# Sample attention: VectorE and ScalarE one pair of slots behind TensorE, and VectorE copying two of four page banks

## What is computed

```
def mla_attend(q_lat, q_pe, ckv, kpe, ckv_past, kpe_past):
    ...
        sp = (jnp.einsum('bqhr,bkr->bhqk', ql, ckv_past)
              + jnp.einsum('bqhd,bkd->bhqk', qp, kpe_past)).astype(jnp.float32) * MLA_SCALE
        p = jax.nn.softmax(jnp.concatenate([sp, s], axis=-1), axis=-1).astype(ckv.dtype)
    ...
def peer(h, w_q, sub_keys, u_tab, v_tab):
    ...                      # top 16 of 16384 experts, for 8 heads
        act = jax.nn.gelu(jnp.einsum('td,thkd->thk', xb, u_tab[ib]), approximate=False) * gb
        return jnp.einsum('thk,thkd->td', act, v_tab[ib])
```

## Time and profile before

| | us |
|---|---|
| median of 3 runs | 3596.35 |
| lowest, highest | 3595.26, 3619.91 |
| the profiled execution | 3605.23 |
| its span | 3603.4 |

### The profile page before, as it was taken

The page is one execution under the profiler, slowest core; times in us unless marked ns, Lnnn a source line. Parts: engine busy times, 40 slices in busy tenths (PEclk is TensorE's granted clock), DMA queues, the critical chain, the costliest instruction groups (busy, mean ns, idle before and its releaser), DMA issues. The chain is left out here.

```text
span 3603.4 us, 44291 instructions
## 1 busy us (share of the span) xinstructions
PE 2576.4 (71%) x15271; PEld 1136.2 (32%) x15271; DVE 2175.5 (60%) x5407; ACT 1593.2 (44%) x4435; POOL 1195.2 (33%) x1114
## 2 busy tenths in 40 slices
PE   8987776666788875766656888866767666656566
PEld 7644222111334432322232443422323322221121
DVE  4863667767776776545345778866454454455566
ACT  3122444444555663244433557744444444444344
POOL 0210444444443443333213344433222222222343
PEclk9988776766898997776777999988888778776687
DMA  4115999999999999898759999999888788888998
GB/s 158 46 32 190 411 426 426 422 427 427 418 400 421 422 420 396 359 370 308 278 214 384 408 421 421 423 406 368 328 330 302 288 309 304 294 295 314 417 426 362
DMA packets 215854, 1240.70 MB, mean 344 GB/s; under 512 B 28015, under 2 KB 63503, under 8 KB 72773
## 3 DMA queue, kind: packets, MB, share of 16 engines
q0 software_dynamic: 154368, 1128.34, 77.5%
q1 hardware_dynamic: 59965, 108.63, 8.2%
q10 hardware_dynamic: 1296, 0.90, 0.1%
HBM read 1233.79 MB, written 4.46 MB: 344 GB/s over the span
## 5 line engine op out<-in xcount | busy, mean ns | idle before, releaser
L1782 PE MATMUL p_acc<-p_rows,p_diag 64*64 64x512 f32 x8192 | 1390.5, 791 | 865.7 <-ACT p_diag L1303 850.3
L1177 POOL DMA_INDIRECT p_rows<-in_peer_uv,p_ids x1024 | 1102.3, 1076 | 2036.6 <-PE p_acc L1782 1886.7
L1569 DVE CUSTOM_DVE_ANT_0 p_rows<-p_rows,p_x_n 128x1024 f32<-128x1024 f32 x1040 | 1248.5, 1221 | 491.6 <-DMA p_rows<-in_peer_uv,p_ids 479.5
L1782 PEld LDWEIGHTS p_acc<-p_rows,p_diag 64*64 64x64 f32 x8192 | 288.3, 159 | 1655.2 <-ACT p_diag L1303 1477.5
L1297 ACT ACTIVATE p_acts<-p_dots 128x1 f32<-128x1 f32 x1040 | 209.2, 201 | 1038.7 <-DVE p_dots L1569 1035.0
L1303 ACT ACTIVATE p_diag<-p_unit,p_gated 128x64 f32<-128x64 f32 x1024 | 356.0, 348 | 33.5
L1299 ACT ACTIVATE p_gated<-p_acts,p_gates 128x1 f32<-128x1 f32 x1024 | 301.7, 295 | 33.3
L1717 PE MATMUL p_q_banks<-p_xT,p_w_q 128*128 128x256 f32 (+3 forms) x1152 | 245.0, 374 | 22.9 <-DMA p_keys<-in_keysT 14.5
L1717 PEld LDWEIGHTS p_q_banks<-p_xT,p_w_q 128*128 128x128 f32 x1152 | 210.1, 204 | 57.9 <-issue 30.9
L1297 ACT ACT_TABLE_LOAD x142 | 182.2, 1283 | 5.9 <-DVE p_dots L1569 3.4
L2665 DVE TENSOR_REDUCE s_peak<-r_bank 128x1 f32<-128x256 f32 x32 | 13.6, 424 | 178.3 <-PE r_bank L2854 178.3
(11 more groups left out here) (417 smaller groups left out, 2787.3 us busy)
## 6 DMA issues: line engine op xcount, KB each, us to landing
p_w_q<-in_w_q_heads SPq DMA_DIRECT2D x35, 1024.0 KB
p_rows<-in_peer_uv,p_ids POOLq DMA_INDIRECT x1024, 14.2
r_arena<-in_c_w_out SPq DMA_DIRECT2D x8, 1024.0 KB, 24.7
a_w_in<-in_ab_w_in SPq DMA_DIRECT2D x6, 1024.0 KB, 11.7
r_arena<-in_w_qx SPq DMA_DIRECT2D x16, 384.0 KB, 12.6
r_arena<-in_c_w_in SPq DMA_DIRECT2D x2, 2688.0 KB, 13.0
r_arena<-in_w_q_heads SPq DMA_DIRECT2D x5, 1024.0 KB, 23.8
p_keys<-in_keysT SPq DMA_DIRECT2D x35, 128.0 KB
```

The costliest lines, as they stand in the source:

```text
L1177: nc.gpsimd.indirect_dma_start(out=rows[:, slot % RING, :], out_offset=None, in_=w[f"peer_uv{layer}"], in_offset=bass.IndirectOffsetOnAxis ...
L1569: nc.vector.tensor_tensor_reduce(rows[:, k % RING, 0:D_MODEL], rows[:, k % RING, 0:D_MODEL], x, 1.0, 0.0, ALU.mult, ALU.add, dots[:, slot ...
L1782: last = nc.tensor.matmul(acc[64 * c:64 * c + 64, 512 * r:512 * r + 512], diag[of, slot // GROUP % 4, j, :], rows[of, (slot + j) % RING, a ...
```

## The change

- The step lists of VectorE and ScalarE for the sample attention begin with one empty step. From then on each is one pair of slots behind TensorE's: what TensorE writes behind pair h, they take behind pair h + 1.
- `turn_weights` and `weighted` move one step later (to steps 4 + 1 and 5 + 1), and with them `weights_out` and `add_piece`, which thereby come two pairs later than before.
- VectorE copies both right-hand page banks (steps 0 and 1); ScalarE's `right_page_out` is gone. The two semaphores for the right bank become one.
- The merge comes one step later, uses `banks[1]` (the right-hand bank) and not `banks[2]`; its waits are on the page copies, and the next `turn_pages` of the right bank waits for it, not `scores`.
- The output of layer 1's round comes one step later; layer 0's round has two steps more, so that its last steps run after the last pair.

The diff, cut to its core:

```diff
-        assert att["stages"] + smp_att["stages"] <= GROUPS * (NW - ROUND_AT if layer == 0 else SMP_X)
+        assert att["stages"] + smp_att["stages"] < (GROUPS * (NW - ROUND_AT) + 4 if layer == 0 else GROUPS * SMP_X)
...
-    OUT_AT = LAST_AT + 11
-    STAGES = LAST_AT + 10 if rnd == 0 else OUT_AT + 7
+    OUT_AT = LAST_AT + 12
+    STAGES = LAST_AT + 12 if rnd == 0 else OUT_AT + 7
...
-    top_row, bias_col, total_col, fold_out = banks[2][0:1, 0:128], banks[2][:, 0:1], banks[2][:, 0:1], banks[2][:, 0:2 * H_C]
+    top_row, bias_col, total_col, fold_out = banks[1][0:1, 0:128], banks[1][:, 0:1], banks[1][:, 0:1], banks[1][:, 0:2 * H_C]
...
-        return SETUP + 4 * last + 6 + step * (4 if last + 1 < NPC else 1)
+        return SETUP + 4 * last + 7 + step * (4 if last + 1 < NPC else 1)
...
-            if rnd == 1 and s == LAST_AT + 6:
+            if rnd == 1 and s == LAST_AT + 7:
                 sp.wait_ge(o_ps, NPC)
...
-        def right_page_out(p):
-            act.wait_ge(right_ps, 2 * p + 2)
-            nc.scalar.copy(pagesT[:, :, 6:8, :], banks[1][:, :].rearrange("p (c s n) -> p c s n", c=2, s=2)).then_inc(right_act, 1)
...
+        yield
         for s in range(STAGES):
...
-            if (p := piece_at(s, 4)) is not None:
+            if (p := piece_at(s, 5)) is not None:
                 weights_out(p)
...
-        def page_out(p):
-
-            dve.wait_ge(right_ps, 2 * p + 1)
+        def page_out(p, r):
+
+            dve.wait_ge(right_ps, 2 * p + r + 1)
             if p:
                 dve.wait_ge(s_ps, p)
-            nc.vector.tensor_copy(pagesT[:, :, 2:4, :], banks[1][:, :].rearrange("p (c s n) -> p c s n", c=2, s=2)).then_inc(right_dve, 1)
+            nc.vector.tensor_copy(pagesT[:, :, 4 * r + 2:4 * r + 4, :], banks[1][:, :].rearrange("p (c s n) -> p c s n", c=2, s=2)).then_inc(right_out, 1)
...
+        yield
         for s in range(STAGES):
...
-            if (p := piece_at(s, 5)) is not None:
+            if (p := piece_at(s, 6)) is not None:
                 add_piece(p)
-            if (p := piece_at(s, 0)) is not None:
-                page_out(p)
+            for r in range(2):
+                if (p := piece_at(s, r)) is not None:
+                    page_out(p, r)
...
-            if r == 1:
-                pe.wait_ge(right_dve, p + 1)
-            elif p:
-                pe.wait_ge(right_act, p)
-            turn_page(banks[1], p, 4 * r + 2, right_ps)
...
+            if p or r:
+                pe.wait_ge(right_out, 2 * p + r)
+            if r == 0 and p > PAST_PIECES:
+                i, step = divmod(p - PAST_PIECES - 1, PAST_PIECES)
                 if step == 0:
                     pe.wait_ge(mx_ready, i + 1)
...
         def turn_top(i):
-            pe.wait_ge(o_used, outs_before(i, 0))
+            pe.wait_ge(top_step, 3 * (PAST_PIECES * i + PAST_PIECES))
+            pe.wait_ge(right_out, 2 * turned_before(i, 0))
...
-            if (p := piece_at(s, 4)) is not None:
+            if (p := piece_at(s, 5)) is not None:
                 turn_weights(p)
-            if (p := piece_at(s, 5)) is not None:
+            if (p := piece_at(s, 6)) is not None:
                 weighted(p)
```

More of the change, by code:

```diff
@@ L1102, in buffer_of, with hooked @@
             return x_n[:, t % 3, :]
-        def hooked(n):
+        def hooked(n, g):
             return n >= ROUND_AT if layer == 0 else n < SMP_X
@@ L1146, in _ @@
                         sp.dma_start(keys[:, 0].rearrange("p c n -> p (c n)"), w["keysT"][layer][:, D_KEY * (H_P - 1):D_KEY * H_P]).then_inc(w_q_in[0], 16)
-                    if n >= 0 and hooked(n):
+                    if n >= 0 and hooked(n, g):
                         next(steps, None)
@@ L1196, in _ @@
                     gather(first_slot(n) + k, ids[:, n % (AHEAD + 1), k:k + 1])
-                    if hooked(n) and k % GROUP == GROUP - 1:
+                    if k % GROUP == GROUP - 1 and hooked(n, k // GROUP):
                         next(steps, None)
@@ L1407, in _ @@
                         exps(route_no(m))
-                    if hooked(n):
+                    if hooked(n, g):
                         next(steps, None)
@@ L2450, in sample_round @@
         oT_ps, oT_ready, y_ps, y_used = sem("oT_ps"), sem("oT_ready"), sem("y_ps"), sem("y_used")
-    left_ps, left_out, right_ps, right_act, right_dve, qpb_ready = (sem(n) for n in (
-        "left_ps", "left_out", "right_ps", "right_act", "right_dve", "qpb_ready"))
+    left_ps, left_out, right_ps, right_out, qpb_ready = (sem(n) for n in (
+        "left_ps", "left_out", "right_ps", "right_out", "qpb_ready"))
     s_ps, top_step, e_ready, pT_ps, pT_ready, o_ps, l_step, o_used = (sem(n) for n in (
@@ L2477, in merge_at, with turned_before @@
         return None
-    def outs_before(i, step):
-        return min(PAST_PIECES * i + PAST_PIECES + step, NPC)
+    def turned_before(i, step):
+        return min(PAST_PIECES * i + PAST_PIECES + 1 + step, NPC)
     def old_top(p):
@@ L2612, in scalar_steps @@
                     left_page_out(p, r)
-            if (p := piece_at(s, 1)) is not None:
-                right_page_out(p)
             if (p := piece_at(s, 2)) is not None:
@@ L2813, in turn_pages @@
             turn_page(banks[0], p, 4 * r, left_ps)
-            if r == 1:
-                pe.wait_ge(right_dve, p + 1)
-            elif p:
-                pe.wait_ge(right_act, p)
+            if p or r:
+                pe.wait_ge(right_out, 2 * p + r)
+            if r == 0 and p > PAST_PIECES:
+                i, step = divmod(p - PAST_PIECES - 1, PAST_PIECES)
+                if step == 0:
+                    pe.wait_ge(mx_ready, i + 1)
+                if step == 1:
+                    pe.wait_ge(bias_out, i + 1)
+                if step == 2:
+                    pe.wait_ge(inv_step, 2 * i + 1)
+                if step == 3:
+                    pe.wait_ge(olT_ready, i + 1)
             turn_page(banks[1], p, 4 * r + 2, right_ps)
@@ L2829, in scores @@
             pe.wait_ge(left_out, 3 * p + 3)
-            pe.wait_ge(right_act, p + 1)
-            pe.wait_ge(right_dve, p + 1)
+            pe.wait_ge(right_out, 2 * p + 2)
             pe.wait_ge(qpb_ready, p // PAST_PIECES + 1)
@@ L2836, in scores @@
                 pe.wait_ge(self_ready, 1)
[L2837 to L2846, removed]
             b = ROUND_SEQS[p // PAST_PIECES]
@@ L2878, in spread_top @@
             pe.wait_ge(nmx_ready, i + 1)
-            pe.wait_ge(o_used, outs_before(i, 1))
+            pe.wait_ge(right_out, 2 * turned_before(i, 1))
             nc.tensor.matmul(bias_col, nmx[:].rearrange("p j h -> p (j h)"), one[:], start=True, stop=True).then_inc(bias_ps, 1)
@@ L2885, in total_sums @@
             pe.wait_ge(consts_in, 48)
-            pe.wait_ge(o_used, outs_before(i, 2))
+            pe.wait_ge(right_out, 2 * turned_before(i, 2))
             nc.tensor.matmul(total_col, fold[:], share[:, 2:3], start=True, stop=True).then_inc(total_ps, 1)
@@ L2890, in fold_heads @@
             pe.wait_ge(on_ready, i + 1)
-            pe.wait_ge(o_used, outs_before(i, 3))
+            pe.wait_ge(right_out, 2 * turned_before(i, 3))
             for c in range(2):
```

## The result

| | before | changed | ratio, 95% interval |
|---|---|---|---|
| median us | 3605.38 (4 runs) | 3296.99 (4 runs, 3291.43 to 3300.95) | 0.9141, 0.9100 to 0.9182 |
| span of the profiled execution, us | 3603.4 | 3295.1 | |

The change made the kernel 8.6% faster. The forecast had the direction and the mechanism, but its time of 3355 us is 58 us too long, and the low end of its range, 3300 us, lies 3 us above the measured median. The kernel before was measured at 3605.38 us in this comparison, 9 us over the 3596.35 that the forecast started from, so the saving was 308 us and the forecast's 242: it is 66 us short.

A forecast was written before the change was run, and what follows sets the result against it. Sample-attention stages were taken as bound by mutual engine waits, not transfers. 279 saved at 420 GB/s, less 48, plus 14, less 3 gives 242 us off 3605.2, so 3363 profiled, 3354 as median, stated 3355; range 3300 to 3435.

The forecast's parts named there:

- The circle: Sample attention: VectorE and TensorE wait for each other in turn, 8.2 us a pair; with the lag this stops setting the pace.
- the list of signs: Layer 1's stage: VectorE's waits from 340 to under 100 us, gather waits, 390 GB/s or more, about 600 us, clock 0.85 or higher.
- TensorE's room and imperfect overlap: 48 us given back: 16 blocks holding the pieces: 3 us lost each; bounds nothing at clock 0.92, about 6 us per query block at the old clock.
- The transfers' floor: 279 us: Both sample stages at 420 GB/s: layer 1's saves 212 us, layer 0's 67, the most this edit can give.
- VectorE's second copy: Sample attention: 22 us more on VectorE, hidden under the transfers; 22 us if that cover is gone.
- `weighted` a pair later: GpSimd's gather of past rows waits for this later step: 0 taken, at most 96 us.
- Merge and the end of layer 0: Last merge of each round saves 7 us, 14 in all; layer 0's steps after the last pair lose 3 us.
- Half of the waits stay: Sample stages: lag too short, TensorE's 358 us of waits for diagonals only halve; 179 us saved, 3417 us; chance 0.16.
- 370 GB/s: Sample stages can't move bytes at 420, only 370 to 376 GB/s at DMA share 1.0; 3407 us; chance 0.12.
- The wait moves to `exps`: ScalarE's `exps`, waiting for VectorE at its own pair, holds the next diagonals and keeps TensorE late; 3585 us; chance 0.05.
- GpSimd held: Gather of past rows waits for `weighted` behind a late TensorE, expert gathers queue behind, slots run dry; 3780 us; chance 0.03.
- The rule on HBM's 358 GB/s: Both sample stages: HBM binds at about 358 GB/s a core; 145 us saved, time near 3490 us; not taken.

The follow-up runs named there:

- e4: Changed kernel with the one-pair lag taken from ScalarE's steps except `exps`, VectorE's kept: 3375.66 us, 0.9305 of the kernel before.
- e5: Changed kernel without the lag for VectorE's page copies, `maxima`, `add_piece` and three merge steps, ScalarE's kept: 3611.84 us, 0.9955 of the kernel before.
- e6: Changed kernel with 26 of the 32 gathers of past rows each replaced by a 2 KB transfer: 3226.33 us, 71 us under the changed kernel.
- e7: Kernel before with the same 26 gathers of past rows left out: 3609.12 us, 1.0009 of the kernel before.
- e10: Changed kernel with each page transpose done four times: 3293.15 us, 0.9144 of the kernel before.
- e11: Changed kernel with a ring of 6 gather buffers instead of 8: 3411.20 us, 0.9468 of the kernel before.
- e1: Changed kernel with the second right-hand page copy given back to ScalarE, lag kept: 3298.07 us, 0.9095 of the kernel before.
- e2: Kernel before with both right-hand page copies on VectorE and no lag: 3674.68 us, 1.0130 of the kernel before.
- e3: Changed kernel with `turn_weights`, `weighted`, `weights_out` and `add_piece` one step earlier, the first two at steps 4 and 5: 3292.98 us, 0.9136 of the kernel before.
- e8: Changed kernel with each page transpose done twice: 3292.53 us, 0.9130 of the kernel before.
- e9: Kernel before with each page transpose done twice: 3667.56 us, 1.0161 of the kernel before.

## Why the prediction was right in kind and too cautious in size

- *The circle.* Right. VectorE's waits for TensorE fell from 340.6 us to 35.5, as the list of signs had asked (under 100), waits for gathers appeared, the rate is 424, the round 555 us, the clock 0.88. Taking either lag away brings waits and time back (e4, e5), and e6 with e7 shows that the bound changed to the transfers. Two readings were loose: VectorE had one wait for a gather in layer 1's stage (0.6 us) where I said none, and of "slices 18 to 20" the first runs at 370 GB/s, outside the 278 to 330 given.
- *TensorE's room and imperfect overlap: 48 us given back.* This is the step that failed: the runs show 0. I read "89% of 575" and "46.6 of 47.5 us in a block with queries" as no room. But 46.6 us do fit into 47.5; the 6 us of the dearer bound are what the experts' matmuls of a block cost more at the lower clock, not a time by which a block overran, and 3 us a block is half of that. Two things were wrong behind it. TensorE can be busy 92% of a stage and cost nothing (e10: 510 us of 554). TensorE's bursts in the blocks with queries are carried by the ring of 8 buffers (with 6 buffers those blocks take 26 us more, e11). And its work did not stay as long as it was: the slots 736 to 927 had TensorE busy 506.46 us before and 438.01 us after, while the granted clock went from 0.80 to 0.88. By e10 the first would probably have been enough. The rows for it were there: 88% busy, clock 0.97 and 422 GB/s in the earlier trace rows. I had cited them as one bound and then averaged with the other.
- *What the sum gives without it.* With 0 in place of the 48 the same sum saves 290 us and gives 3306, inside the range. The spans differ by 308. Of the 18 us left, 13 are in layer 0's round, as said next, 2 in layer 1's (221 against 212 + 7) and 3 outside both. That 3306 comes within 9 us of the measured 3297 is in part luck, since the kernel before ran 9 us longer in this comparison than in the forecast's rows.
- *The transfers' floor: 279 us.* The right bound, priced too low, and not "the most that this edit can give": the two rounds gave 305. The rate came out at 424 and not 420 (242 MB over 424 are 570 us and not 575), and I had cut layer 0's stage to its pieces (259 us). The 93 us of its round ahead of them already ran below the full rate:

```profile
1464.00:1557.00 93.00, 58.45 (x412) 18.59 (x416) 51.69 (x129) 31.98 (x102) 34.17 (x33) 0.73 0.94 386
```

With them its six blocks went from 352 to 268 us: 84 us, where the terms for layer 0 come to 67 + 7 - 3 = 71.
- *VectorE's second copy.* Right: hidden (e1), and a cost where its cover is gone, 48 us without the lag (e2), more than the 22 us I named; the rest of the 48 was not explained.
- *`weighted` a pair later.* Right at 0: GpSimd waited for it at most 0.5 us, 6 times, and e3, which brings it one step forward again, has the same time.
- *Merge and the end of layer 0.* About right: what VectorE still does of the merge after its last sum into `x_sb` takes about 2 us, from the reciprocal at 1758.11 to the end of the last copy at 1760.21; I had said 3.

```profile
1755.30 2.78 DVE L1584 TENSOR_TENSOR x_sb<-x_sb,p_acc 64x512 f32<-64x512 f32 x4
1758.11 0.17 DVE L2704 RECIPROCAL s_share<-r_bank 128x1 f32<-128x1 f32 x1
...
1759.99 0.22 DVE L2715 COPY smp_olT<-r_bank 128x32 f32<-128x32 f32 x1 [1.12 <-PE r_bank L2888]
```

- *The rivals.* "Half of the waits stay": no. Of VectorE's waits for TensorE 10% stayed. Of TensorE's waits for diagonals, by which this rival was priced, 37% did (100.4 of 268.5 us), but those no longer set the pace. "370 GB/s": no, and its argument was a misreading: the DMA share does not grow in proportion to the rate (below). "The wait moves to `exps`": its 113.5 us became 29.5. "GpSimd held": no.
- *The rule on HBM's 358 GB/s* (the Trainium skill, DMA: Bandwidth & Descriptors, "Where 436 GB/s comes from"): the stage that decides runs at 424, so the trace goes against it again, and with it 3490 us. The section of the Trainium skill just above that one ("Measured (HBM→SBUF, 128 partitions, SWDGE, issued from GpSimd)") gives about 358 GB/s as what each core gets when both cores of a pair stream. This kernel runs on one core, so the forecast weighed the rule without its condition.

What stays open: e8 and e10 have medians 4 us under the changed kernel's, which was itself timed only in the first comparison; whether a higher clock gains anything was not settled. Nor was what the moved copy costs beyond its own time in e2.

## What to carry to other kernels

Where a step of one engine is hung behind a shared piece of work and another engine takes its result behind the same piece, the taker waits for everything that the first has ahead of it; take the result one piece of that shared work later, above all on the engine whose next work starts everybody else's. Read whether the transfers bind by leaving bytes out, and whether an engine has room by giving it more of the same work: both say more than a busy share. When the rows hold a stage with the same structure, as full and at full rate, price by that stage and not by the middle between it and a worse one.

## What the runs showed of the hardware

- *The DMA share is no scale for the rate.* Layer 1's round, in different kernels of this study: 0.78 with 287 GB/s (e9), 0.80 with 299 (e5), 0.83 with 307 (before), 0.94 with 371 (e4), 0.98 with 403 (e11), 1.01 with 424 (changed). From 0.83 to 1.01 (22%) the rate grows by 38%. An extrapolation of the share to 1.0 gave 370, which was 54 too low.
- *More transposes alone raised TensorE's clock in the changed kernel*, from 0.88 to 0.99 with four times as many (e10). The clock has two levels, 1.2 and 2.4 GHz, so by an estimate from these means the higher one was granted for 76% and then 98% of the time. The 0.92 with twice as many (e8) shows little, as e1 has 0.91 with no more transposes than the changed kernel. In the kernel before, where TensorE waits between its steps, twice as many raised nothing: 0.79 against 0.80 (e9). The Trainium skill (TensorE: Matmul & The Clock Gate, "Part 4: PE-mode transpose") says that the full clock does not engage for transposes. In e10, where float32 transposes stand among matmuls, it came closer to full with them.
- *The kernel before seems less steady than the changed one.* Its median was 3600 to 3630 us in the different comparisons; the changed kernel and e1, whose layer 1 rounds are alike, gave 3297 and 3298, though each was timed in one comparison only.
